# Paired projection loads, long decay reads, copies moved ahead, and half of the SSM output projection in split fp32r, in a hybrid decoder step on one core

## The chip, the core and the metric

The kernel runs on one core of one Trainium2 chip. The metric is the device time of one execution in microseconds; three executions of the kernel before give a median of 1370.95 us. Everything told below of the inside of an execution comes from one profiled execution.

## What is computed

One inference step of one layer for 256 prompt tokens and 8 sample tokens (264 rows, D_MODEL 1024, all float32): one wide input projection, a Mamba-2 state-space branch and a dilated window attention branch side by side, a gated sum of both, and a mixture of experts (top 4 of 32).

```python
def token_mixer(u, conv_buf, h0, kv_bufs, is_prompt, w_in, conv_w, conv_b, dt_bias, a_log, d_skip,
                ssm_norm_g, w_out_ssm, w_out_attn, w_out):
    proj = u @ w_in                                  # 9472 columns and dt
    z, xbc, dt_raw, q, k, v, gate_a, gate_b = jnp.split(proj, cuts, axis=-1)
    xbc_c = jax.nn.silu(causal_dwconv(xbc_ext, conv_w, conv_b))
    ...
    y, h_new = ssd_scan(xs, dt, A, Bm, Cm, h0)       # h0: (8, 32, 64, 128) for the samples
    y = (y + d_skip[:, None] * xs).reshape(Bsz, T, D_INNER) * jax.nn.silu(z)
    branch_a = group_rms_norm(y, ssm_norm_g) @ w_out_ssm          # 2048 x 1024
    ...                                              # attention: s = q k^T * scale - slope * dist, masked
    merged = jax.nn.sigmoid(gate_a) * branch_a + jax.nn.sigmoid(gate_b) * branch_b
    return merged @ w_out, new_conv, h_new, new_kv
```

Besides the result rows, the step returns the new convolution tail, the new sample states (8 MiB) and the sample caches moved on by one row: the latter is a plain copy of 44 MB in DRAM.

## The kernel before

**Projection (0 to 285 us).** w_in is taken in 37 units u of 256 columns. A unit is one 1 MiB load (L421) into `wraw`, a ring of RING = 5 places; its rows in DRAM are 1 KB long. A unit gives two tiles m = 2u, 2u+1 of 128 columns. A tile is made by ACT's rounded copy `high` (L799, into `wh`), the rest `wlow` by DVE (L1179) or GpSimd (L688), and 24 TensorE matmuls in fp32r (L1904 to L1906: xh by wh, xl by wh, xh by wlow). `tile_done` counts finished tiles. All weight loads are issued by SyncE (SP) from one list in program order; before the load of u it waits for `tile_done` >= 2(u-5)+2, which frees the place.

Between the loads the same list holds everything else that SP moves: a piece of the cache copy (`move_cache`, L432; 48 pieces, 40 of them of 1.05 MB, 8 of 0.26 MB), the broadcast reads of the decays (`decay_in`, L445: `a_scratch` in DRAM to `acb`, 0.5 MB), from u = 17 the sample inputs' round trip (`x_scratch` write L507, `xdts` read L509), and the sample states (`state_in` L462, `state_back` L467, 1 MiB each). An instruction of SP that waits holds all behind it.

**State-space phase, within the projection, from about 98 us.** Eight steps `it`, a group and a chunk each, run with the tiles from 26 on. For each sample b DVE makes the new state (L1324 once, then L1328, L1331) and reads it out (L1337, L1338). The states stand in `hs`, a ring of two: state_in(b) waits for the landing of state_back(b-2) (`hs_out`). PE's spread of the B and C rows of sample b waits for `hs_read` of b-1. The first of these DVE steps needs `xdts`, which has come back from DRAM.

**Attention and w_out_ssm (285 to 385 us).** `from_ssm(n)`, n = 0 to 15 (L2106), is a quarter of w_out_ssm's contraction for a pair of output tiles: four k, two column tiles, 8 float32 matmuls of 128x264 which the trace holds as 16 records. They are placed between the scores (L2089, L2090), the turned weights (L2122) and the products with the values (L2133 to L2135). Weights come by `native(i)` (L540) into `wnat`, again five places of 1 MiB. DVE adds a slope times distance (`bias`, L1436) to each head's scores (L1439), reduces them, and multiplies the sample queries with cached keys (L1486 to L1491); GpSimd scales the weights (L725). The masks are made at 256 to 272 us (L1391 to L1397). Values of the sample caches (`vsel`) are loaded by ACT (L971).

**Behind it.** `native(12)`, a quarter of w_out, waits for `native_used` = 8, that is for the end of from_ssm(15); behind it in SP's list stand the first weight chunks of the experts (L574, 2 MiB each). The output mix (L2243), norm and router follow to about 440 us, and the expert blocks to the end.

## Time and profile before

| | |
|---|---|
| median of 3 runs (lowest, highest) | 1370.95 us (1370.46, 1373.19) |
| profiled execution: time, span | 1370.5 us, 1368.8 us |
| granted clock, mean | 0.992 |
| PE, DVE, ACT, GpSimd busy | 1308.8, 574.5, 296.7, 169.9 us |
| DMA | 539.93 MB, mean 394 GB/s |

The span is the time from the first to the last instruction that the profiler saw; the 1.7 us between it and the execution's time lie around it. The shares are means over stages with different limits, so the stages above are read apart: the busy times in a window, the chain of work that ended last in it, and for a queue its issues in order of time.

### The profile page before, as it was taken

How to read it: one execution, taken by the hardware profiler on the slowest of the kernel's cores; microseconds unless marked ns; L12 is line 12 of the kernel's file. 1: busy time of each engine (PE TensorE's matmuls, PEld its weight loads, DVE VectorE, ACT ScalarE, POOL GpSimd, SP SyncE). 2: the span in 40 equal slices, each digit the busy share in tenths (PEclk: the TensorE clock that was granted, in tenths of full speed). 3: DMA queues.
4: the chain of work that ended last, by engine and by line, in shares of the span. 5: the costliest groups of instructions: out<-in, count | busy, mean ns of one | idle time of the engine just before them, and what ended most of it. 6: DMA issues, size and time to landing. Idle time of an engine off the chain costs nothing.

```text
span 1368.8 us, 24720 instructions
## 1 busy us (share of the span) xinstructions
PE 1308.8 (96%) x10213; PEld 653.0 (48%) x10213; DVE 574.5 (42%) x896; ACT 296.7 (22%) x603; POOL 169.9 (12%) x232
## 2 busy tenths in 40 slices
PE   9998999999999999999999999999999999999996
PEld 7998899976765333333333333333333322333322
DVE  4988999878457322132223221112222122222114
ACT  6778665643211100000000000000000000000002
POOL 1006774404000000000000000000000000000000
PEclk9999999999999999999999999999999999999998
DMA  8998998999999999999999999999999999999994
GB/s 269 338 386 258 359 364 294 380 345 383 400 375 369 396 424 428 425 427 427 429 426 427 428 427 429 424 428 424 428 427 428 428 427 427 426 429 425 431 424 189
DMA packets 113637, 539.93 MB, mean 394 GB/s; under 512 B 12901, under 2 KB 76501, under 8 KB 80773
## 3 DMA queue, kind: packets, MB, share of 16 engines
q1 hardware_dynamic: 103866, 524.91, 94.8%
q10 hardware_dynamic: 8448, 9.83, 2.2%
q0 software_dynamic: 1264, 4.35, 0.8%
q8 instruction: 44, 0.72, 0.2%
q14 instruction: 15, 0.12, 0.0%
HBM read 522.69 MB, written 60.56 MB: 426 GB/s over the span
## 4 chain that ended last, share of the span: by engine, by line
PE 64%; DMA 26%; DVE 6%; issue 2%; ACT 1%; POOL 1%; SPq 0%; ACTq 0%; DVEq 0%; POOLq 0%
PE psum L2394 21%; DMA wnat<-in_w_down_dram 10%; PE psum L2417 10%; DMA wmx<-in_w_down_dram 8%; DMA whm<-in_w_down_dram 6%; PE psum L2380 5%; PE psum L1904 4%; PE psum L1905 4%; PE psum L1906 4%; PE psum L2106 3%; PE psum L2440 3%; PE psum L2444 2%; PE psum L2243 1%; DMA x_scratch<-xbc 1%; PE psum L2425 1%
## 5 line engine op out<-in xcount | busy, mean ns | idle before, releaser
L1779 DVE STREAM_TRANSPOSE hturn<-psum 128x1024 f32<-128x1024 f32 x32 | 40.0, 1250 | 402.6 <-PE psum L2394 402.6
L1904 PE MATMUL psum<-xh,wh 128*128 128x264 f32 x592 | 173.1, 292 | 3.8 <-ACT zz L829 3.2
L1906 PE MATMUL psum<-xh,wlow 128*128 128x264 f32 x592 | 168.5, 285 | 0.0
L1905 PE MATMUL psum<-xl,wh 128*128 128x264 f32 x592 | 168.3, 284 | 0.0
L1116 ACT ACTIVATE sg<-hb 128x512 f32<-128x512 f32 x32 | 20.2, 631 | 523.5 <-DVE hb L1788 523.5
L2394 PE MATMUL psum<-wmh,xst 128*32 128x512 f32 x1056 | 118.6, 593 | 0.9 <-DVE xst L1745 0.8
L762 POOL COPY gcol<-gm 128x3 f32 (+1 forms) x32 | 17.4, 543 | 811.0 <-DVE hb L1783 810.3
L1904 PEld LDWEIGHTS psum<-xh,wh 128*128 128x128 f32 x592 | 112.3, 190 | 10.7 <-ACT zz L829 4.8
L1905 PEld LDWEIGHTS psum<-xl,wh 128*128 128x128 f32 x592 | 112.4, 190 | 1.4 <-issue 1.4
L1906 PEld LDWEIGHTS psum<-xh,wlow 128*128 128x128 f32 x592 | 111.7, 189 | 0.0
L2417 PE MATMUL psum<-wnat,hst 128*64 128x512 f32 x400 | 91.6, 598 | 14.3 <-DMA wnat<-in_w_down_dram 10.9
L2394 PE MATMUL psum<-spare,xst 128*32 128x512 f32 x816 | 95.1, 593 | 0.0
L2380 PE MATMUL psum<-x,oneh 128*32 128x256 f32 x1488 | 91.1, 390 | 0.0
L688 POOL TENSOR_TENSOR wlow<-wraw,wh 128x1024 fp32r<-128x1024 f32 x28 | 73.4, 2641 | 124.0 <-ACT wh L799 124.0
L2394 PE MATMUL psum<-wnat,xst 128*32 128x512 f32 x752 | 85.1, 592 | 0.0
L799 ACT ACTIVATE wh<-wraw 128x1024 fp32r<-128x1024 f32 x73 | 76.8, 1054 | 1.0 <-DMA wraw<-in_w_in_dram 1.0
L2380 PEld LDWEIGHTS psum<-x,oneh 128*32 128x32 f32 x1488 | 46.3, 108 | 54.2 <-issue 24.9
L2394 PEld LDWEIGHTS psum<-wmh,xst 128*32 128x32 f32 x1056 | 33.3, 110 | 75.5 <-issue 71.7
L1799 DVE TENSOR_TENSOR hst<-hu,sg 128x512 f32<-128x512 f32 x31 | 21.5, 693 | 110.4 <-PE psum L2417 110.4
L2417 PEld LDWEIGHTS psum<-wnat,hst 128*64 128x64 f32 x400 | 28.0, 136 | 77.7 <-issue 65.6
L2106 PE MATMUL psum<-zz,wnat 128*128 128x264 f32 x256 | 62.9, 400 | 0.0
L2440 PE MATMUL psum<-orow,gtok 64*128 64x512 f32 x248 | 61.6, 615 | 0.0
(459 smaller groups left out, 1733.2 us busy)
## 6 DMA issues: line engine op xcount, KB each, us to landing
wmh<-in_w_gate_up_dram SPq DMA_DIRECT2D x33, 2048.0 KB, 34.8
spare<-in_w_gate_up_dram SPq DMA_DIRECT2D x21, 2048.0 KB, 30.5
wnat<-in_w_gate_up_dram SPq DMA_DIRECT2D x20, 2048.0 KB, 36.9
wnat<-in_w_down_dram SPq DMA_DIRECT2D x20, 2048.0 KB, 34.8
wraw<-in_w_in_dram SPq DMA_DIRECT2D x37, 1024.0 KB, 9.9
out_dram<-in_cache_kv_w_dram SPq DMA_DIRECT2D x32, 1023.5 KB, 11.7
whm<-in_w_gate_up_dram SPq DMA_DIRECT2D x12, 2048.0 KB, 35.6
wmx<-in_w_gate_up_dram SPq DMA_DIRECT2D x11, 2048.0 KB, 37.5
```

The costliest lines, as they stand in the source:

```text
L688: g.tensor_tensor(half_of(wlow, m), half_of(wraw, m), high_of(m).bitcast(F32), ALU.subtract).then_inc(S("low_pool"), 1)
L799: a.activation(high_of(m), half_of(wraw, m), ACT.Copy).then_inc(S("high_done"), 1)
L1779: v.transpose(hturn[:, :].rearrange("p (f c i) -> p f c i", c=4, i=QW), psum[:, at:at + 2, :].rearrange("p h (f i c) -> p (h f) c i", c=4, ...
L1904: mm(out, hi[:, k, :], xh[:, k, :], start=(k == 0), stop=False)
L1905: mm(out, hi[:, k, :], xl[:, k, :], start=False, stop=False)
L1906: last = mm(out, lo[:, k, :], xh[:, k, :], start=False, stop=(k == KT - 1))
L2106: last = mm(bank[6 + odd][:, 0:T], w[:, k, odd * P:(odd + 1) * P], zz[:, KT * (r // 2) + k, :], start=(r == 0 and k == 0), stop=(r == 3 an ...
L2380: last = mm(bank[at][q * QW:(q + 1) * QW, 256 * h:256 * h + 256], rows_[:, t, h * QW:(h + 1) * QW], of_quarter(t, q), start=(t == 0), stop ...
L2394: last = mm(bank[at + h][q * QW:(q + 1) * QW, :], x_rows[:, h, k, :], w[:, q, :, :, :], start=(k == 0), stop=(k == KT - 1))
L2417: last = mm(bank[at][BLK * half:BLK * half + BLK, :], rows_[:, k, :, :].rearrange("p h r -> p (h r)"), w[:, col:col + 512], start=(k == 0) ...
L2440: last = mm(bank[3 + 2 * t + half], tok[rows_, t * P:(t + 1) * P], out[rows_, :], start=first, stop=final)
L2444: last = mm(bank[7][0:BLK, :], sam[:, :], out[:, :], start=first, stop=final)
```

## The change

1. *Paired loads.* For 2 <= u < 32 with u % 5 < 4, units (2,3), (5,6), (7,8), (10,11), ... (30,31) are one 2 MiB load, with DRAM rows of 2 KB; the others stay single. The place of a pair is two neighbours in the ring, so the pair's load waits until the *second* of the places is free.
2. *Long decay reads.* `a_scratch` is laid out so that a decay read is one 4 KB row per partition instead of eight of 512 B; it is written by four DMAs instead of one.
3. *Copies.* Every unit from 18 on has a piece of the cache copy (before: the even ones, and those above 33): 30 pieces instead of 22 are in the projection, 18 instead of 26 behind it (two instead of three behind native(0) to (4), one instead of two behind native(5) to (7)).
4. *w_out_ssm.* 8 of the 16 calls of `from_ssm` (n = 2, 3, 6, 7, 10, 11, 14, 15) are split: ACT rounds the weights (`wsh`) and, in two instructions, half of the normed rows (`zhi`); DVE makes the rests (`wlow`, `zlo`); PE does 24 fp32r matmuls instead of 8 float32 ones. from_ssm(8) stands before the loop over heads, and 9 to 11 one place later.
5. *Scores.* The masks hold the distance, and the slope goes into the scale of the exponential, so the 12 `bias` instructions go.
6. *Sample values* (`vsel`) are loaded by GpSimd behind its 12 scalings of `pa`, after `qk_done` 8. Some buffers lie elsewhere, and some semaphores are merged.

```diff
+        def load_of(u):
+
+            return u - u % RING % 2 if 2 <= u < 32 and u % RING < 4 else u
+
+        def units_of(u):
+
+            return 2 if load_of(u + 1) == u else 1
+
+        def raw_ready(eng, u):
+
+            n = load_of(u)
+            loads = sum(load_of(v) == v for v in range(n % RING, n + 1, RING))
+            eng.wait_ge(S(f"raw_landed{n % RING}"), 16 * loads)
...
@@ -441,8 +497,8 @@
                 gi, c = divmod(it, 2)
                 if it >= 3:
                     sp.wait_ge(S("ssd_y"), it - 2)
-                src = a_scratch[gi * HPG:(gi + 1) * HPG, c * P:(c + 1) * P].unsqueeze(0).broadcast_to([P, HPG, P])
-                sp.dma_start(acb[:, it % 3, :, :], src).then_inc(S(f"acb_in{it % 3}"), 16)
+                src = a_scratch[gi, c].rearrange("h l -> (h l)").unsqueeze(0).broadcast_to([P, HPG * P])
+                sp.dma_start(acb[:, it % 3, :, :].rearrange("p h l -> p (h l)"), src).then_inc(S(f"acb_in{it % 3}"), 16)
...
                 if u >= RING:
-                    sp.wait_ge(S("tile_done"), 2 * (u - RING) + 2)
-                    if 5 < u < 17 or u > 33 or (u >= 18 and u % 2 == 0):
+                    before = u + units_of(u) - 1 - RING
+                    sp.wait_ge(S("tile_done"), 2 * (load_of(before) + units_of(load_of(before)) - 1) + 2)
+                    if 5 < u < 17 or u > 17:
                         move_cache(next(pieces))
-                load(u, wraw[:, u % RING, :].rearrange("p (k n) -> p k n", k=KT), w_in_v[:, :, w_in_col(u):w_in_col(u) + 256])
+                if load_of(u) == u:
+                    load(u, raw_place(wraw, u), w_in_v[:, :, w_in_col(u):w_in_col(u) + 256 * units_of(u)])
...
-                    sp.wait_ge(S("a_out"), 16)
+                    sp.wait_ge(S("a_out"), 16 * GROUPS)
...
             for i in range(RING):
                 native(i)
-                for _ in range(3):
+                for _ in range(2):
                     move_cache(next(pieces))
...
             for i in range(RING, N_SSM + N_ATT + N_OUT):
                 native(i)
                 move_cache(next(pieces))
-                if i < N_SSM:
-                    move_cache(next(pieces))
```

In attention and w_out_ssm:

```diff
+        SSM_SPLIT = (2, 3, 6, 7, 10, 11, 14, 15)
...
+            def ssm_split(n):
+
+                native_ready(act, n // 2)
+                at = SSM_SPLIT.index(n)
+                if at == 2:
+                    act.wait_ge(*reached("rstd_ready"))
+                elif at > 2:
+                    ssm_used(act, SSM_SPLIT[at - 3])
+                a.activation(ssm_high(n), ssm_part(wnat, n), ACT.Copy).then_inc(S("high_done"), 1)
...
+                own.then(v.scalar_tensor_tensor(out=mk, in0=mk, scalar=NEG, in1=rel[:, :], op0=ALU.mult,
+                                                op1=ALU.subtract))
...
+            def norm_low(gi):
+
+                high_ready(dve, f"z{gi}")
+                v.tensor_tensor(zlo[:, 4 * gi:4 * gi + 4, :], zz[:, 4 * gi:4 * gi + 4, :],
+                                zhi[:, 4 * gi:4 * gi + 4, :].bitcast(F32), ALU.subtract).then_inc(S("low_done"), 1)
+
+            def ssm_low(n):
+
+                high_ready(dve, f"w{n}")
+                v.tensor_tensor(ssm_part(wlow, n), ssm_part(wnat, n), ssm_high(n).bitcast(F32),
+                                ALU.subtract).then_inc(S("low_done"), 1)
...
-                bs = bias[:, h % 2, :]
-                own.then(v.scalar_tensor_tensor(out=bs, in0=rel[:, :], scalar=-SLOPES[h], in1=masks[:, h // HG, :],
-                                                op0=ALU.mult, op1=ALU.add))
+                if h in (1, 3):
+                    norm_low(2 + h // 2)
+                elif h in (2, 4):
+                    ssm_low(1 + h // 2)
+                elif h == 8:
+                    ssm_low(6)
                 dve.wait_ge(S("scores_psum"), h + 1)
-                v.scalar_tensor_tensor(out=pa[:, h, :], in0=bank[4 + h % 2][:, 0:3 * P], scalar=SCALE, in1=bs,
-                                       op0=ALU.mult, op1=ALU.add).then_inc(S("score_read"), 1)
+                v.scalar_tensor_tensor(out=pa[:, h, :], in0=bank[4 + h % 2][:, 0:3 * P], scalar=SCALE / SLOPES[h],
+                                       in1=masks[:, h // HG, :], op0=ALU.mult, op1=ALU.add).then_inc(S("score_read"), 1)
                 dve.wait_ge(S("score_read"), h + 1)
...
+                if n in SSM_SPLIT:
+                    low_ready(pe, f"w{n}")
+                    hi, lo = (w.rearrange("p (k n) -> p k n", k=4) for w in (ssm_high(n), ssm_part(wlow, n)))
+                else:
+                    native_ready(pe, n // 2)
+                    w = ssm_part(wnat, n).rearrange("p (k n) -> p k n", k=4)
                 for odd in range(2):
-                    for k in range(4 * (r % 2), 4 * (r % 2) + 4):
-                        last = mm(bank[6 + odd][:, 0:T], w[:, k, odd * P:(odd + 1) * P], zz[:, KT * (r // 2) + k, :],
-                                  start=(r == 0 and k == 0), stop=(r == 3 and k == KT - 1))
-                if r % 2:
-                    last.then_inc(S("native_used"), 1)
+                    out, cols = bank[6 + odd][:, 0:T], slice(odd * P, (odd + 1) * P)
+                    for k in range(4):
+                        f = 4 * r + k
+                        if n not in SSM_SPLIT:
+                            last = mm(out, w[:, k, cols], zz[:, f, :], start=(f == 0), stop=False)
+                            continue
+                        mm(out, hi[:, k, cols], zhi[:, f, :], start=(f == 0), stop=False)
+                        mm(out, hi[:, k, cols], zlo[:, f, :], start=False, stop=False)
+                        last = mm(out, lo[:, k, cols], zhi[:, f, :], start=False, stop=(f == ZT - 1))
+                last.then_inc(S("native_used" if r % 2 else "half_used"), 1)
...
+            from_ssm(8)
             keys = [min(P, PAST // d) for _, d in DIL]
             for n in range(NH + 1):
                 if n == 4:
@@ -2181,7 +2282,7 @@
                     weights_turn(n)
                 if n:
                     weights_times_v(n - 1)
-                if n in (2, 5, 8, 11):
+                if n in (3, 6, 9):
                     from_ssm(8 + n // 3)
```

SP's list around the sample inputs' round trip (x_scratch), before: the loads are u = 15, then 16, then 17, then 18.

```order
L432 DMA out_dram<-in_cache_kv_w_dram 16x16352 [waits tile_done]
L421 DMA wraw<-in_w_in_dram 128x8x256
L421 DMA wraw<-in_w_in_dram 128x8x256 [waits tile_done]
L507 DMA x_scratch<-xbc 128x16x8 [waits conv_done]
L509 DMA xdts<-x_scratch 128x128 [waits xs_out]
L432 DMA out_dram<-in_cache_kv_w_dram 16x4064 [waits tile_done]
L421 DMA wraw<-in_w_in_dram 128x8x256
```

And of the change, from the pair (15, 16) to the copy of u = 18:

```order
L488 DMA out_dram<-in_cache_kv_w_dram 16x16376 [waits tile_done]
L477 DMA wraw<-in_w_in_dram 128x8x512
L488 DMA out_dram<-in_cache_kv_w_dram 16x16352 [waits tile_done]
L477 DMA wraw<-in_w_in_dram 128x8x512 [waits tile_done]
L565 DMA x_scratch<-xbc 128x16x8 [waits conv_done]
L567 DMA xdts<-x_scratch 128x128 [waits xs_out]
L488 DMA out_dram<-in_cache_kv_w_dram 16x4064 [waits tile_done]
```

The load ahead of `x_scratch` is now the pair (17, 18), and it waits for tile 27; before it was the single u = 17, which waited for tile 25.

SP's list at the sample states, before: from the load of u = 20 to that of u = 23, with the states 2 in, 1 back and 3 in.

```order
L421 DMA wraw<-in_w_in_dram 128x8x256
L462 DMA hs<-in_state_ssm_dram 128x2048 [waits hs_out0,hs_read]
L421 DMA wraw<-in_w_in_dram 128x8x256 [waits tile_done]
L445 DMA acb<-a_scratch 128x8x128 [waits ssd_y]
L467 DMA out_dram<-hs 128x2048 [waits hnew_ready]
L432 DMA out_dram<-in_cache_kv_w_dram 16x16376 [waits tile_done]
L421 DMA wraw<-in_w_in_dram 128x8x256
L462 DMA hs<-in_state_ssm_dram 128x2048 [waits hs_out1,hs_read]
L421 DMA wraw<-in_w_in_dram 128x8x256 [waits tile_done]
```

And of the change, from the copy of u = 20 (the loads are (20, 21) and (22, 23)):

```order
L488 DMA out_dram<-in_cache_kv_w_dram 16x16376 [waits tile_done]
L477 DMA wraw<-in_w_in_dram 128x8x512
L518 DMA hs<-in_state_ssm_dram 128x2048 [waits hs_out0,hs_read]
L488 DMA out_dram<-in_cache_kv_w_dram 16x16376 [waits tile_done]
L501 DMA acb<-a_scratch 128x1024 [waits ssd_y]
L523 DMA out_dram<-hs 128x2048 [waits hnew_ready]
L488 DMA out_dram<-in_cache_kv_w_dram 16x16376 [waits tile_done]
L477 DMA wraw<-in_w_in_dram 128x8x512
L518 DMA hs<-in_state_ssm_dram 128x2048 [waits hs_out1,hs_read]
```

State 3 in (the last row) now stands behind a copy and a pair that wait for `tile_done` 38; before, behind a copy and a single load that waited for 36.

ACT's list in the attention stage, before: the end of the prompt's softmax (L1007, L1009), then the scalings (L1015) and the copies of the turned weights (pT, L1029).

```order
L1007 ACT_TABLE_LOAD
L1007 ACTIVATE ast<-ast 128x24 [waits aexp_done]
L1009 ACT_TABLE_LOAD
L1009 ACTIVATE ast<-ast 128x24 [waits dve_stage]
L1015 ACTIVATE pa<-pa,ast 128x128 [waits dve_stage]
L1015 ACTIVATE pa<-pa,ast 128x128 x2
L1029 ACTIVATE pT<-psum 128x384 [waits pturn_psum]
L1015 ACTIVATE pa<-pa,ast 128x128
```

And of the change: the roundings for from_ssm(10), (11) and (14) (L1041) stand in it.

```order
L1078 ACT_TABLE_LOAD
L1078 ACTIVATE ast<-ast 128x24 [waits aexp_done]
L1041 ACTIVATE wsh<-wnat 128x1024 [waits native_used,native_landed2]
L1081 ACT_TABLE_LOAD
L1081 ACTIVATE ast<-ast 128x24 [waits dve_stage]
L1087 ACTIVATE pa<-pa,ast 128x128 [waits dve_stage]
L1087 ACTIVATE pa<-pa,ast 128x128
L1041 ACTIVATE wsh<-wnat 128x1024 [waits half_used,native_landed2]
L1041 ACTIVATE wsh<-wnat 128x1024 [waits native_used,native_landed4]
L1087 ACTIVATE pa<-pa,ast 128x128
L1100 ACTIVATE pT<-psum 128x384 [waits pturn_psum]
```

The rounding for from_ssm(10) stands ahead of the softmax's last exponential, those for 11 and 14 ahead of the first pT, and each waits for its piece of w_out_ssm: native(5) (`native_landed2`) and native(7) (`native_landed4`).

## Rows read from the trace of the kernel before

**Rows 1.** Windows: busy us by engine, TensorE clock, DMA share, GB/s
```profile
106.00:108.00 2.00, 1.62 (x14) 1.41 (x12) 1.23 (x1) 1.97 (x3) 0.00 (x0) 1.00 0.66 112
120.00:220.00 100.00, 97.33 (x854) 89.59 (x853) 99.44 (x81) 66.31 (x124) 78.79 (x29) 1.00 1.02 353
320.00:380.00 60.00, 58.72 (x350) 44.38 (x348) 32.24 (x81) 14.34 (x33) 12.84 (x14) 1.00 1.04 407
...
480.00:1340.00 860.00, 828.54 (x6641) 273.41 (x6636) 199.16 (x272) 55.20 (x150) 41.85 (x116) 1.00 1.01 427
```

**Rows 2.** Chain that ended last, 285 to 395 us: start, us, what
```profile
288.40 3.76 PE psum L2106 x16
...
308.92 0.56 DVE bias L1436
...
329.04 3.76 PE psum L2106 x16
...
363.48 0.71 DVE gates L1425
...
385.22 9.54 DMA wnat<-in_w_out_dram
```

**Rows 3.** The same chain at 96 to 112 us
```profile
96.18 1.96 SPq L421
98.18 11.93 DMA x_scratch<-xbc
110.12 1.81 DMA xdts<-x_scratch
```

**Rows 4.** PE in order of time, first work behind tile 27
```profile
103.44 1.06 PE L2007 MATMUL psum<-bcrow,ident 32*32 32x256 f32 x16
```

**Rows 5.** SP in order of time: start, us of issue, what
```profile
146.59 0.35 SPq L462 DMA_DIRECT2D hs<-in_state_ssm_dram  x1
150.66 0.37 SPq L421 DMA_DIRECT2D wraw<-in_w_in_dram  x1
...
168.88 2.53 SPq L467 DMA_DIRECT2D out_dram<-hs  x1
175.34 0.52 SPq L432 DMA_DIRECT2D out_dram<-in_cache_kv_w_dram  x1
...
178.62 0.34 SPq L462 DMA_DIRECT2D hs<-in_state_ssm_dram  x1
```

**Rows 6.** DMA issues at 146 to 147 us: KB each, us to landing
```profile
hs<-in_state_ssm_dram SPq DMA_DIRECT2D x1, 1024.0 KB, 9.5
```

**Rows 7.** DMA issues at 16 to 17 us, nothing queued ahead
```profile
wraw<-in_w_in_dram SPq DMA_DIRECT2D x1, 1024.0 KB, 5.4
```

**Rows 8.** DVE in order of time: the start and three sample states
```profile
112.03 2.39 DVE L1324 TENSOR_TENSOR xdts<-xdts,feat 128x128 f32<-128x128 f32 x1 [1.49 <-DMA xdts<-x_scratch]
...
116.78 2.35 DVE L1331 SCALAR_TENSOR_TENSOR hs<-hs,feat,sprod 128x2048 f32<-128x2048 f32 x1
...
161.00 3.48 DVE L1331 SCALAR_TENSOR_TENSOR hs<-hs,feat,sprod 128x2048 f32<-128x2048 f32 x1
...
192.91 3.87 DVE L1331 SCALAR_TENSOR_TENSOR hs<-hs,feat,sprod 128x2048 f32<-128x2048 f32 x1
```

**Rows 9.** Groups by line: busy us, mean ns, idle before and releaser
```profile
L1179 DVE TENSOR_TENSOR wlow<-wraw,wh 128x1024 fp32r<-128x1024 f32 x45 | 55.8, 1260 | 5.3 <-ACT wh L799 5.2
...
L1439 DVE SCALAR_TENSOR_TENSOR pa<-psum,bias 128x384 f32<-128x384 f32 x12 | 6.7, 557 | 7.7 <-PE psum L2090 7.5
L1436 DVE SCALAR_TENSOR_TENSOR bias<-rel,masks 128x384 f32<-128x384 f32 x12 | 6.6, 552 | 0.0
```

**Rows 10.** PE in order of time: one tile, 25 records of a steady stretch
```profile
59.74 0.28 PE L1904 MATMUL psum<-xh,wh 128*128 128x264 f32 x1
...
62.64 0.28 PE L1904 MATMUL psum<-xh,wh 128*128 128x264 f32 x1
```

**Rows 11.** DVE in order of time: the last step of a mask
```profile
260.48 0.36 DVE L1397 TENSOR_SCALAR masks<-masks 128x384 f32<-128x384 f32 x1
```

More of the change, by code:

```diff
@@ L590, in _ @@
             for m in range(10):
[L591 to L593 removed]
+                if m == 2:
                     sp.wait_ge(S("native_used"), N_SSM)
@@ L1246, in convolve @@
                     if m < CW - 1:
-                        steps.then(last)
+                        own.then(last)
                 t = ctmp[:, u % 3, :, TP:T]
```

163 lines of the change are left out of this document (98 added, 65 removed).

## The prediction

> **What bounds the kernel now.** I read the windows first, then the chain of waits, then the queues in order of time. The windows [rows 1] show three regimes. At 120 to 220 us everything is full: PE 97.33 and DVE 99.44 of 100 us, DMA share 1.02 at 353 GB/s. At 320 to 380 us PE is busy 58.72 of 60. From 480 us on DMA has share 1.01 at 427 GB/s, so the expert stage can't be shortened from here; it can only start sooner or later. Its gate is in the chain [rows 2]: behind the end of from_ssm(15) at 385.22 us comes the wait of 9.54 us for a piece of w_out, and the first expert chunks are issued behind that piece. So the kernel's end moves with the end of from_ssm(15), microsecond for microsecond. Fewer bytes ahead of that gate don't move it, since it is PE's. The change therefore has to be summed over two stretches: the projection (to 285 us) and attention with w_out_ssm (285 to 385 us).
>
> **Attention and w_out_ssm.** *Split products.* A call of from_ssm takes 3.76 us (16 records) [rows 2]. 24 fp32r matmuls of the same width take 62.64 - 59.74 = 2.90 us [rows 10]. That is 0.87 us less, and 8 x 0.87 = 7.0 us of PE's time. But the chain is on DVE from about 307 us (a `bias` step at 308.92) to 329.04 [rows 2]. Ahead of it, n = 2 and 3 bring the scores 1.7 us sooner. In the DVE stretch the splits of n = 6 and 7 are hidden; DVE loses four `bias` steps (chain at 308.92 and its like, 0.55 us each by [rows 9]: -2.2) and gets two `ssm_low` of the kind of L1179, 1.26 us [rows 9]: +2.5. Together -1.7 - 2.2 + 2.5 = **-1.4 us**. The other eight `bias` steps lay in DVE's waits for PE (L1439 waits 7.5 us for L2090 [rows 9]), and the four other rests (2 x 1.3 and 2 x 1.26 = 5.1 us) go where they were. From 329 us PE bounds, and n = 10, 11, 14, 15 give 4 x 0.87 = **-3.5 us**, if their halves are ready. ACT makes each from a piece that must have landed; if it is late, ACT holds the exponential and the copies queued behind it, and DVE and PE wait for these. One or two MB less behind each native piece make it likely that (5) and (7) are in time; a piece that is 2 us late costs 2 us. from_ssm(8) to (11) moved ahead of DVE's waits: the chain's piece at 363.48 (gates, 0.71 us [rows 2]) is partly filled, **-0.5 us**. Sum: -5.4. Bounds: all PE time saved and the gap filled, 7.0 + 1.5 = -8.5; only the four late ones, half of them on time, and the lows exposed, -3.
>
> GpSimd's loads of the sample values start behind its scalings, some 22 us later than ACT's first; their reader at 372 us is still 15 us or more behind the landing. I take 0; if it fails, it costs the same wait at from_ssm(14), at most 3 us. DVE's rests now run beside GpSimd. L1331 takes 2.35 us at 116.78 and 3.48 at 161.00 [rows 8], where GpSimd is busy most of the time (78.79 of 100 us [rows 1]). The Trainium skill, "SBUF - State Buffer", section "Who interferes with whom", says why: a DVE instruction with two SBUF inputs and a GpSimd instruction that reads SBUF exclude each other. By it `ssm_low(10)`, which meets the scalings at 325 to 337 us, could wait for one of them, 1 us; the sum does without.
>
> The masks' last step becomes one with two inputs: 0.55 (as L1436 [rows 9]) for 0.36 [rows 11], three times, +0.6 us, on the chain at 256 to 272 us.
>
> **Projection, what is removed.** Rows of 2 KB and 4 KB. A 1 MiB load with nothing ahead lands in 5.4 us [rows 7]; the full queue moves 353 GB/s with short rows, 427 with long ones [rows 1]. Between these a MiB costs 2.97 or 2.46 us, so a pair saves between 0 and 1.0 us of the queue. 12 pairs: 0 to 12 us of DMA time, the decays' reads another 0 to 3. Against it stand 8 more copy pieces in u = 19 to 33, 6 x 1.05 + 2 x 0.26 = 6.8 MB, 19 us at 353 GB/s, where the share is 1.02 already. So the queue is by 4 to 19 us busier there, not freer. The Trainium skill ("DMA: Bandwidth & Descriptors", section "Anatomy of one DMA") gives about 2.0 us plus bytes by 436 GB/s for a DMA issued by GpSimd. By it a pair takes 6.8 us where two single loads in a row take 8.8, and the change would win. The trace speaks for it only where the queue is empty, and there it is not.
>
> **Projection, what is added: waits.** A pair waits for its second place, two tiles later than its first unit did, and what stands behind it on SP waits too.
>
> (a) *Start.* The pair (2,3) lands as one. The first two slots' tiles wait for 2 MiB instead of 1: 2.5 us at 427 GB/s, of which ACT's other work hides a part. **+1.5 us** (0 to 2.5).
>
> (b) *x_scratch.* Before, SP issued u = 17 at 96.18, x_scratch at 98.18, landing 11.93 us later, and xdts follows at 110.12 with 1.81 [rows 3]; DVE starts at 112.03 after idling [rows 8]. The queue's payload ended near 106.6, as the 112 GB/s at 106:108 shows [rows 1]: x_scratch lands 3.5 us behind it. In the change the pair (17,18) waits for tile 27, and the first PE work behind tile 27 is at 103.44 [rows 4]. 2 MiB at 353 to 427 GB/s is 4.9 to 5.9 us, with 2 us to its start (5.4 less the 2.5 to 3 us of its bytes) it ends at 110.3 to 111.4. +3.5 for x_scratch, +1.9 for xdts gives 116.3, against 112.03: **+4.3 us** (3 to 6). DVE has no idle time from here to 220 us, so nothing takes it back. What is late next: PE's spread for samples 1 and on, all in step.
>
> (c) *States.* State 3 in is issued at 146.59 behind tile_done 36 and lands after 9.5 us [rows 5, 6], at 156.1; DVE uses it at 161.00 [rows 8]: 4.9 us of slack. In the change it stands behind tile_done 38, when SP took u = 23 before (150.66 [rows 5]), and behind a copy and 2 MiB, 3.1 MB or 7.4 to 8.9 us, and its own 1 MiB, 2.5 to 3: 161.9 to 163.5 plus up to 2 of landing: +1 to +4.5. State 3 back goes from 168.88 to behind 175.34, +6.5, and state 5 in needs its landing (178.62 before [rows 5]). 178.62 + 6.5 + 9.5 = 194.6, against the use at 192.91 [rows 8]: +1.7, more if queues are longer. State 6: +0.7 to 2.8 in the same way. PE is within 3% of being the bound here and can run ahead by one sample, so some of it is won back: **+3.5 us** (0 to 8).
>
> Projection: 1.5 + 4.3 + 3.5 + 0.6 = **+9.9 us** (3 to 17).
>
> **Sum.** 9.9 - 5.4 = +4.5 us on the profiled execution's 1370.5: **1375.0 us**. That execution is 0.45 us under the median of 1370.95, less than the runs' own spread.
>
> **The rivals.**
> A, *delays outweigh the splits* (forecast): 1372 to 1379, from +7 to +14 in the projection.
> B, *faster*. The delays are absorbed: the queue, emptier at 98 to 104 us by the pair's late issue, takes the 2 MiB at once, and long rows keep the states' latencies below 9.5 us, so that state 3 meets its 4.9 us. Left are 1.5 + 0.6 and at most 1.5 of (b): 1370.5 + 3.6 - 5.4 = 1368.7, with the ends of the gains 1365 to 1362.5. It decides if xdts lands before 113.5 us and DVE keeps its 99% at 120 to 220. For it: a pair's two units are there in one piece, and PE can wait little. Against it: x_scratch's fixed place behind tile 27. This is also where the skill's rule of "DMA: Bandwidth & Descriptors" points.
> C, *they cancel*: (b) in full, no state late: 1.5 + 4.3 + 0.6 - 5.4 = +1.0, 1371.5.
> D, *the queue is the bound*: the 19 us of added copies come back as late states at each of three turns, and ACT waits for weights at 250 us: +17 - 5.4, 1382.
> That the change does not do what it says I exclude for the splits and the order: the lists show them.
>
> **Chances.** A 0.44, B 0.33, C 0.13, D 0.10. A measurement of this kernel can tell about 0.2%, 2.7 us. Faster than 1368.2: 0.32 (B nearly whole); within: 0.21 (C and A's low end); slower than 1373.7: 0.47. The range 1362.5 to 1384 leaves out the tails of B and D. Since B has another sign, A's own range: 1371 to 1380.
>
> **What would show it.** x_scratch issued near 104.5 and DVE's L1324 at 116, not 112. DVE idle for `hs` ahead of its fourth and sixth L1331; DVE under 97% at 120 to 220 us. DMA over 353 GB/s there. End of the projection (the first scores) near 295 instead of 285. 8 calls of from_ssm at 2.9 us, and from there to the w_out wait 95 us instead of 100. The experts' stage unchanged in length. Wrong would be: no idle of DVE for states (then B or C), a gain under 3 us behind the projection (ACT held by a native piece), or an expert stage of other length.

## The result and the profile after

The changed kernel takes **1391.85 us** (median of 4 runs, 1391.47 to 1394.32) for 1370.7 us; the ratio is 1.0154 (1.0136 to 1.0172). It is slower by 21 us. I had forecast 1375.0 and a range of 1362.5 to 1384: the sign was right and the size was far too small.

Windows of the changed kernel (busy us of PE, PEld, DVE, ACT, GpSimd, then TensorE's clock, DMA share, GB/s):

```profile
22.00:30.00 8.00, 6.85 (x56) 6.51 (x55) 3.60 (x5) 4.65 (x7) 0.00 (x0) 1.00 0.60 201
30.00:60.00 30.00, 27.95 (x221) 27.51 (x220) 27.32 (x62) 21.18 (x41) 0.00 (x0) 0.94 0.73 265
125.00:235.00 110.00, 105.25 (x885) 97.50 (x886) 94.05 (x83) 70.68 (x130) 78.16 (x29) 0.95 0.94 346
330.00:335.00 5.00, 5.00 (x14) 3.76 (x15) 4.72 (x16) 3.52 (x13) 3.11 (x4) 0.53 1.29 465
480.00:1340.00 860.00, 828.19 (x6654) 271.84 (x6644) 203.13 (x275) 55.86 (x151) 44.77 (x124) 1.00 1.01 426
```

The kernel before, in the first two of these:

```profile
22.00:30.00 8.00, 8.00 (x68) 7.71 (x65) 5.10 (x8) 7.85 (x16) 0.00 (x0) 1.00 1.10 348
30.00:60.00 30.00, 29.53 (x246) 29.14 (x246) 28.32 (x61) 23.07 (x43) 0.00 (x0) 1.00 1.01 343
```

The row 480:1340 answers to that in [rows 1]: share 1.01 at 426 GB/s for 427, so the expert stage is as it was. At 22 to 60 us the DMA queue is not full any more: share 0.60 and 0.73 for 1.10 and 1.01. At 125 to 235 us DVE is busy 94.05 of 110 us; the kernel before had it at 99.44 of 100 at 120 to 220 us. The share is 0.94 there, though there was more to move.

SP of the changed kernel in order of time, with the places that answer to [rows 3] and [rows 5]:

```profile
107.65 0.38 SPq L477 DMA_DIRECT2D wraw<-in_w_in_dram  x1
108.07 0.58 SPq L565 DMA_DIRECT2D x_scratch<-xbc  x1
119.08 0.34 SPq L567 DMA_DIRECT2D xdts<-x_scratch  x1
...
141.67 0.54 SPq L488 DMA_DIRECT2D out_dram<-in_cache_kv_w_dram  x1
142.25 0.58 SPq L477 DMA_DIRECT2D wraw<-in_w_in_dram  x1
142.94 0.51 SPq L518 DMA_DIRECT2D hs<-in_state_ssm_dram  x1
...
145.23 0.45 SPq L523 DMA_DIRECT2D out_dram<-hs  x1
...
163.62 0.33 SPq L518 DMA_DIRECT2D hs<-in_state_ssm_dram  x1
```

The pair (17,18) is issued at 107.65 where I had put it at 104, and the write of the round trip behind it has landed by 119.08 for 110.12. In the state ring, write-back 1 goes at 145.23 and state 3 can only be asked for at 163.62. These are the DMA pieces of over 8 us in the chain that ended last, from 16 to 300 us (start, us, what):

```profile
16.36 9.36 DMA wraw<-in_w_in_dram
...
77.28 12.11 DMA wraw<-in_w_in_dram
...
95.04 14.51 DMA wraw<-in_w_in_dram
...
145.23 18.33 DMA out_dram<-hs
...
163.62 10.40 DMA hs<-in_state_ssm_dram
...
205.28 14.72 DMA out_dram<-hs
...
221.68 14.66 DMA out_dram<-hs
...
236.40 8.33 DMA hs<-in_state_ssm_dram
...
254.72 9.51 DMA y_scratch<-ysum
```

Up to 110 us the chain waits three times for weights, and the round trip of x_scratch is not in it; then it goes through the ring of states, and at the end through a second round trip (y_scratch, the samples' y), whose write takes 9.51 us to land. The write-back at 145.23 takes 18.33 us to land (8.9 to 12.5 for the eight of the kernel before), behind a copy, a 2 MiB load, a state, a second copy and a decay read, all issued within 4 us ahead of it. Who waited on DMA in the first 300 us, DVE first, then ACT (total, times, longest):

```profile
DVE hs L1403 <- DMA hs<-in_state_ssm_dram: 19.8, 5, 4.9
...
DVE xbc L1444 <- DMA ysf<-y_scratch: 5.0, 1, 5.0
```

```profile
ACT wh L858 <- DMA wraw<-in_w_in_dram: 32.0, 11, 6.0
```

In the kernel before, DVE waited neither for a state nor for `ysf`, and ACT once, 1.0 us, for weights. Now DVE waits 19.8 us for states and ACT 32.0 us for weights.

TensorE's clock fell too. It was granted at the lower of its two levels (1.2 of 2.4 GHz) in several stretches, each behind one in which PE had waited; one of them, from 126 us on, is in the chain:

```profile
124.00:128.00 4.00, 1.72 (x8) 1.73 (x9) 4.00 (x3) 3.97 (x6) 0.76 (x1) 0.68 0.63 165
128.00:132.00 4.00, 4.00 (x20) 4.00 (x20) 3.96 (x4) 0.43 (x2) 3.96 (x2) 0.50 0.69 258
```

Added up over windows of 1 us from 18 us to the first score, the granted clock is short of full speed by 12.0 us in the changed kernel, and by 1.7 us in the kernel before. What this adds to the time, beside the waits ahead of it, no run parts.

The traces of all kernels split the time at two places: the first score (L2089 before, L2183 after), and the issue of the last piece of w_out, which SP may do at the end of from_ssm(15).

| kernel | projection, to the first score | first score to end of from_ssm(15) | from there to the end |
|---|---|---|---|
| before | 285.1 | 100.1 | 983.6 |
| changed | 306.9 | 101.1 | 984.6 |

These lengths are of one profiled execution each; that of the changed kernel was its slowest, 1394.32 us for a median of 1391.85. The projection lost 21.8 us. The attention stage, in which I had expected -5.4, lost 1.0. The rest is rigid, as forecast.

### The profile page after: what moved, and what is told of

It reads as the page before. It is cut to its first block, busy times and chain, and to the rows that moved or that the text cites. A ratio compares the mean times of both kernels' runs of the same rounds, so it can differ in the third digit from the quotient of the medians.

```text
span 1392.6 us, 24840 instructions
## 1 busy us (share of the span) xinstructions
PE 1314.6 (94%) x10277; PEld 661.4 (47%) x10277; DVE 571.5 (41%) x894; ACT 306.5 (22%) x613; POOL 169.1 (12%) x235
## 4 chain that ended last, share of the span: by engine, by line
PE 56%; DMA 34%; DVE 5%; ACT 2%; issue 2%; SPq 1%; ACTq 0%; DVEq 0%
PE psum L2495 21%; DMA wnat<-in_w_down_dram 10%; PE psum L2518 9%; DMA wmx<-in_w_down_dram 8%; DMA wmh<-in_w_down_dram 6%; PE psum L2481 5%; DMA out_dram<-hs 3%; PE psum L2541 3%; DMA wraw<-in_w_in_dram 3%; PE psum L1998 2%; PE psum L1999 2%; PE psum L2000 2%; PE psum L2204 2%; PE psum L2545 2%; DMA hs<-in_state_ssm_dram 1%
## 5 line engine op out<-in xcount | busy, mean ns | idle before, releaser
L1998 PE MATMUL psum<-xh,wh 128*128 128x264 f32 x592 | 177.3, 300 | 11.2 <-ACT zz L888 4.0
L1999 PE MATMUL psum<-xl,wh 128*128 128x264 f32 x592 | 171.9, 290 | 0.0
L2000 PE MATMUL psum<-xh,wlow 128*128 128x264 f32 x592 | 171.7, 290 | 0.0
L1998 PEld LDWEIGHTS psum<-xh,wh 128*128 128x128 f32 x592 | 115.8, 196 | 18.9 <-ACT zz L888 5.6
L2495 PE MATMUL psum<-wmh,xst 128*32 128x512 f32 x1088 | 122.0, 593 | 2.7 <-DMA wmh<-in_w_gate_up_dram 1.0
L1999 PEld LDWEIGHTS psum<-xl,wh 128*128 128x128 f32 x592 | 116.1, 196 | 1.4 <-issue 1.4
L2000 PEld LDWEIGHTS psum<-xh,wlow 128*128 128x128 f32 x592 | 115.4, 195 | 0.0
L1253 DVE TENSOR_TENSOR wlow<-wraw,wh 128x1024 fp32r<-128x1024 f32 x45 | 54.2, 1231 | 7.6 <-ACT wh L858 7.4
## 6 DMA issues: line engine op xcount, KB each, us to landing
wraw<-in_w_in_dram SPq DMA_DIRECT2D x12, 2048.0 KB, 11.3
```

The source lines that it names most:

```text
L1253: v.tensor_tensor(half_of(wlow, m), half_of(wraw, m), high_of(m).bitcast(F32), ALU.subtract).then_inc(S("low_done"), 1)
L1998: mm(out, hi[:, k, :], xh[:, k, :], start=(k == 0), stop=False)
L1999: mm(out, hi[:, k, :], xl[:, k, :], start=False, stop=False)
L2000: last = mm(out, lo[:, k, :], xh[:, k, :], start=False, stop=(k == KT - 1))
L2495: last = mm(bank[at + h][q * QW:(q + 1) * QW, :], x_rows[:, h, k, :], w[:, q, :, :, :], start=(k == 0), stop=(k == KT - 1))
```

## Experiments

Two stages, so two questions: what in the projection costs 22 us, and where the split products' gain went. The kernels whose names begin with a are the changed one with something undone, those with b the kernel before with something added. The first four undo or do the pairs and the moved copies. A median is compared with that of the kernel before run beside it (1369.9 to 1370.8 us). The lengths of stages and the waits are of one profiled execution, which lies up to 4.2 us from its kernel's median: above it by 3.1 us in b_pairs_first, 4.2 in b_pairs_last and in b_pairs_x, 4.1 in a_late, below it by 2.6 in a_single_late and 2.1 in a_both.

**a_single**

```diff
         def load_of(u):
-            return u - u % RING % 2 if 2 <= u < 32 and u % RING < 4 else u
+            return u
```

> The changed kernel with single 1 MiB projection loads, each waiting for its own place only (the pairing undone); the 8 moved copies, the long decay reads and everything in the attention stage stay. The change lost 21 us against the kernel before; all of it is in the projection, where the first score stands at 306.9 us for 285.1. Theory P (the pairs' waits and bursts starve the ring of two states): the projection ends near 286 to 289 us and the time is 1371 to 1376, and no L1403 waits for DMA longer than 1 us. Theory C (the 6.8 MB of copies overload a full queue): the state waits stay, 1386 to 1390. Theory B (it takes both): 1377 to 1384.

1377.52 us (1373.62 to 1381.07), ratio to before 1.0046 (1.0025 to 1.0066). 14.3 of the 21 us come back with the pairs. Still 8.1 us of waits for states in three places, so the copies have a part of their own.

**a_copies**

```diff
-                    if 5 < u < 17 or u > 17:
+                    if 5 < u < 17 or u > 33 or (u >= 18 and u % 2 == 0):
                         move_cache(next(pieces))
...
                 native(i)
-                for _ in range(2):
+                for _ in range(3):
...
                 move_cache(next(pieces))
+                if i < N_SSM:
+                    move_cache(next(pieces))
```

> The changed kernel with the cache copies where they were before (22 pieces in the projection, 26 behind it); the pairs stay. Theory P: 1385 to 1390, little regained. Theory C: 1372 to 1376. Theory B: 1377 to 1384. In each, the landing of a state's write-back (14.7 to 18.3 us in the changed kernel, 8.9 to 12.5 before) says how much was queued ahead of it.

1396.07 us (1395.42 to 1400.14): 4 us slower than the changed kernel, which none of the theories had. The two places in its trace say why: first score at 299.1 (7.8 us sooner than changed), but 110.5 us from there to the end of from_ssm(15) for 101.1. The copies are a cost in the projection and a gain behind it; a_both shows the second part more clearly.

**a_both**: both edits.

> The changed kernel with both undone: single loads and the copies as before. What is left is the long decay reads, the split products, the folded slope and the sample values by GpSimd. If the projection is as before, the time is the attention stage's alone: the traces give +1.0 us for it (101.1 us from the first score to the end of from_ssm(15) for 100.1), so 1371 to 1373; my prediction said -5.4 for it, 1366.

1375.22 us (1373.09 to 1376.26), ratio 1.0034 (1.0023 to 1.0045). First score at 282.1, which is 3 us *sooner* than before; then 105.3 us for 100.1. ACT of this kernel in order of time, its roundings for from_ssm(6), (7), (10) and (11) (start, duration, and in brackets the idle time ahead and what ended it):

```profile
298.18 1.06 ACT L1043 ACTIVATE wsh<-wnat 128x1024 fp32r<-128x1024 f32 x1 [7.40 <-DMA wnat<-in_w_out_ssm_dram]
...
303.54 1.04 ACT L1043 ACTIVATE wsh<-wnat 128x1024 fp32r<-128x1024 f32 x1
...
322.48 1.06 ACT L1043 ACTIVATE wsh<-wnat 128x1024 fp32r<-128x1024 f32 x1 [11.11 <-DMA wnat<-in_w_out_ssm_dram]
...
327.01 1.04 ACT L1043 ACTIVATE wsh<-wnat 128x1024 fp32r<-128x1024 f32 x1
```

ACT stands 7.40 and 11.11 us for a piece of w_out_ssm that has not landed. Behind the second stands the last exponential of the softmax; DVE waits for it and PE for DVE, 6.5 us in one piece by PE's list of waits. So with the copies where they were, the change to the attention stage as a whole loses 5.2 us; the moved copies are what makes room for the pieces.

**b_pairs**: the pairs alone, on the kernel before, with the waits and the places of the change.

```diff
-                    sp.wait_ge(S("tile_done"), 2 * (u - RING) + 2)
+                    before = u + units_of(u) - 1 - RING
+                    sp.wait_ge(S("tile_done"), 2 * (load_of(before) + units_of(load_of(before)) - 1) + 2)
...
+                if load_of(u) == u:
+                    load(u, raw_place(wraw, u), w_in_v[:, :, w_in_col(u):w_in_col(u) + 256 * units_of(u)])
```

> The kernel before with the paired loads and nothing else. Theory P: at least three quarters of the projection's loss, +15 us or more, 1386. Theory C: +1 to +5. Theory B: +5 to +12. My prediction's own terms for this part, 1.5 + 4.3 + 3.5 = +9.3, give 1380.

1386.68 us (1385.37 to 1387.92), ratio 1.0118 (1.0102 to 1.0135): +16.0 us, theory P. First score at 299.0, attention 100.1 as before.

**The waits or the transfers.**

b_two_loads:

```diff
                 if load_of(u) == u:
-                    load(u, raw_place(wraw, u), w_in_v[:, :, w_in_col(u):w_in_col(u) + 256 * units_of(u)])
+                    for v in range(u, u + units_of(u)):
+                        load(v, wraw[:, v % RING, :]..., w_in_v[:, :, w_in_col(v):w_in_col(v) + 256])
```

> The kernel before, whose loads wait as the pairs do (for the second place, and what stands behind them in SP's list too), but each pair is two single 1 MiB loads, one right behind the other, each with its own semaphore. Paired loads alone took 1386.7 us for 1370.7. Theory W (the later waits of SP cost it): nearly the same loss, 1382 to 1388. Theory L (the pair lands only as a whole, so ACT gets its first tile late): most comes back, 1371 to 1375. If half each: 1376 to 1381. Rows of 1 KB instead of 2 KB would make it slower by up to 0.5 us a MiB where the queue is full.

1383.48 us (1382.0 to 1385.22), +13.6 of the 16 us (the kernel before beside it took 1369.9). Theory W: most is the waiting for the second place. The other 2.4 us are not clear of noise (1.01, 1.0082 to 1.0117, for 1.0118, 1.0102 to 1.0135). They fit a transfer that lands only as a whole, since ACT waits 16.6 us for weights here and 23.0 in b_pairs, but no run shows that this is their cause; in any case the 2 KB rows gained nothing.

**Which waits.** Three kernels look into b_pairs by place.

b_pairs_first and b_pairs_last change the range of the pairs in b_pairs:

```diff
-            return u - u % RING % 2 if 2 <= u < 32 and u % RING < 4 else u
+            return u - u % RING % 2 if 2 <= u < 15 and u % RING < 4 else u
```

with `20 <= u < 32` in the second. b_pairs_x issues the write of the round trip ahead of the wait for the pair (17,18):

```diff
+                if u == 17:
+                    with nc.allow_non_contiguous_dma(reason="eight tokens"):
+                        sp.wait_ge(S("conv_done"), 12)
+                        sp.dma_start(by_feature(x_scratch), xbc[:, X0:X0 + ZT, TP:T]).then_inc(S("xs_out"), 16)
                 if u >= RING:
                     before = u + units_of(u) - 1 - RING
...
-                        sp.wait_ge(S("conv_done"), 12)
-                        sp.dma_start(by_feature(x_scratch), xbc[:, X0:X0 + ZT, TP:T]).then_inc(S("xs_out"), 16)
                         sp.wait_ge(S("xs_out"), 16)
```

> The kernel before with pairs only for u = 2 to 13; no state and no round trip stands behind one of their waits. All pairs: +16 us. Theory F (the ring of five weight places, refilled by twos, lets ACT and PE run dry in the first 100 us): +6 to +10, 1376 to 1380. Theory S (the loss is in what stands behind the waits, states and round trip): +1.5 to +3, 1371.5 to 1373, the start alone, as I had predicted.

1376.55 us (1375.1 to 1379.61), +6.6 us: theory F for this part. Its ACT, in order of time:

```profile
25.37 1.06 ACT L819 ACTIVATE wh<-wraw 128x1024 fp32r<-128x1024 f32 x1 [3.02 <-DMA wraw<-in_w_in_dram]
...
59.77 1.07 ACT L819 ACTIVATE wh<-wraw 128x1024 fp32r<-128x1024 f32 x1 [2.84 <-DMA wraw<-in_w_in_dram]
...
78.23 1.06 ACT L819 ACTIVATE wh<-wraw 128x1024 fp32r<-128x1024 f32 x1 [3.85 <-DMA wraw<-in_w_in_dram]
...
90.72 1.06 ACT L819 ACTIVATE wh<-wraw 128x1024 fp32r<-128x1024 f32 x1 [3.68 <-DMA wraw<-in_w_in_dram]
...
100.38 1.06 ACT L819 ACTIVATE wh<-wraw 128x1024 fp32r<-128x1024 f32 x1 [1.31 <-DMA wraw<-in_w_in_dram]
...
108.07 1.06 ACT L819 ACTIVATE wh<-wraw 128x1024 fp32r<-128x1024 f32 x1 [3.20 <-DMA wraw<-in_w_in_dram]
```

> The kernel before with pairs only for u = 20 to 31, where the states move. My prediction's term for the states was +3.5 (0 to 8). Theory F: 1371 to 1376. Theory S: +8 to +12, 1378 to 1382. The weights should be in time here, since a tile takes 4 us of PE and DVE for 2.9 in the first 95 us.

1377.13 us (1375.07 to 1381.37), +7.2 us, just under theory S (+8), with 8.8 us of DVE's waits for states in four places, and 4.9 us of ACT's for weights:

```profile
DVE hs L1351 <- DMA hs<-in_state_ssm_dram: 8.8, 4, 5.8
```

> The kernel before with all pairs, and the write of the round trip (x_scratch) issued ahead of the wait and load of the pair (17,18). My price for its delay was 4.3 us: 1386.7 - 4.3 = 1382.4 if it is on the path that sets the end. If PE and ACT, short of weights, are as late as DVE by then, the round trip is covered: 1385 to 1387.

1383.64 us (1382.03 to 1387.88): +13.7 for b_pairs' +16.0, each against the kernel before beside it. These 2.3 us are not clear of noise (1.0097, 1.0081 to 1.0112, for 1.0118, 1.0102 to 1.0135), and the traces speak against them: in b_pairs_x SP asks for xdts at 113.62 and DVE waits for it no more, but DVE's first product with it (`sprod`) starts at 121.17 for 121.60 in b_pairs, and neither chain holds the round trip; both wait for weights up to 109.7 us. So with all pairs the round trip is covered.

The pairs below u = 15 and those from 20 on make 6.6 + 7.2 = 13.8 of the 16.0 us. The other 2.2 belong to the pairs (15,16) and (17,18), which neither kernel has, if the parts add up. Each stretch in which SP stood for a second place lost time, the first of them before any state moved.

**The order of the copies.** If the pieces of the cache copy harm by standing ahead of the states, they may stand behind them:

```diff
-                    if 5 < u < 17 or u > 17:
+                    if 5 < u < 17:
                         move_cache(next(pieces))
...
                 elif u >= 20 and u < 20 + 2 * (TS - HSN):
                     state_in((u - 16) // 2)
+                if u > 17:
+                    move_cache(next(pieces))
```

This edit on a_single is a_single_late, and on the changed kernel a_late.

> Single loads and the moved copies as in a_single (1377.5 us), but from u = 18 on each copy is issued behind that unit's load, decay read and state transfers instead of ahead of them: the same bytes and the same waits in another order. Theory Q (what stands ahead of a state's transfer in SP's list and in its queue delays it): the waits of L1403 for states fall from 8.1 us to under 2, the projection ends 3 to 6 us sooner, 1372 to 1374.5. Theory R (the bytes alone, a full DMA queue): no gain, 1376 to 1379, since the queue is as full.

1371.94 us (1369.36 to 1375.32), ratio 1.0012 (1.0 to 1.0024): 5.6 us less than a_single from the order alone. No DVE step waits for a state, and at 120 to 220 us:

```profile
120.00:220.00 100.00, 97.33 (x847) 89.93 (x847) 99.02 (x85) 66.37 (x124) 78.66 (x29) 0.98 1.03 392
```

392 GB/s, for 353 in [rows 1], with DVE at 99.02. The added bytes went through. The first score stands at 284.7 us for 290.8 in a_single, and 282.1 in a_both without the moved copies: of the 8.7 us that they cost, 6.1 were the order, and 2.6 are left (by one trace each, and that of a_single_late is its fastest).

> The changed kernel (paired loads, moved copies) with the same reordering of the copies from u = 18 on. Theory Q: the copy was 1 MB of the 4 to 5 MB ahead of a state; the pair's 2 MiB and its later wait stay, so about a third of the 21 us comes back, 1384 to 1388. If the pairs' loss is mostly ACT's waits for weights (32.0 us in eleven waits in the changed kernel, 1.0 before), which the copies behind make no better, 1389 to 1393.

1390.09 us (1386.89 to 1394.14): 1.8 us less than the changed kernel, within the noise. With the pairs, ACT still waits 29.7 us for weights and DVE 18.6 for states; the copies' order is not what holds them.

**The attention stage.**

a_single_from8, on a_single:

```diff
                 if b % 2:
                     from_ssm(4 + b // 2)
-            from_ssm(8)
...
-                if n in (3, 6, 9):
+                if n in (2, 5, 8, 11):
                     from_ssm(8 + n // 3)
```

> a_single with from_ssm(8) to (11) at the places of the kernel before (n = 2, 5, 8, 11 of the head loop). In a_single PE waits 3.0 us for the gated sum (L1511) at from_ssm(8), and runs 1.4 us slower behind it at a lower clock. If that place is the cost: -3 to -4.5 us, 1373 to 1374.5. If DVE's later steps bind the stretch anyway: within 1 us of 1377.5.

1375.53 us (1374.33 to 1376.2), 2.0 us less; the stage takes 98.6 us for a_single's 100.8. The new places of from_ssm(8) to (11) were a cost of about 2 us. The two intervals overlap (1.0021 to 1.0043, 1.0025 to 1.0066), but a_best below finds the same 2 us again.

a_single_nosplit, on a_single, all 16 calls in float32, with no roundings and rests:

```diff
-        SSM_SPLIT = (2, 3, 6, 7, 10, 11, 14, 15)
+        SSM_SPLIT = ()
```

> a_single with all 16 calls of from_ssm in float32 matmuls: no ACT roundings and no DVE rests for w_out_ssm; order of calls, folded slope and the rest stay. By my prediction's price of 0.87 us a call, with those for n = 6, 7 hidden and n = 2, 3 half, it is 4 to 5 us slower than a_single: 1382. By the trace of a_single a split call stands for 3.12 us (303.34 to 306.46), 0.64 less than 3.76, and its rests cost DVE 1.2 us each in a stretch that DVE bounds: only n = 10, 11, 14, 15 pay, 2.6 us, and six rests and roundings give back 2.4 to 3.7: 1376 to 1378, the same as a_single.

1378.65 us (1376.51 to 1380.48), with 1377.52 within its range. In the profiled executions the stage takes 103.8 us for 100.8, in the medians the whole differs by 1.1, which is within the noise. My terms for the splits with DVE's rests came to 2.7 us (1.7 - 2.5 + 3.5). The chain of this kernel, from_ssm(4) and (13), both float32:

```profile
317.41 5.91 PE psum L2211 x16
...
376.36 5.44 PE psum L2211 x16
```

**What is left, and a faster kernel.**

a_plain: the changed kernel with the edits of a_single, a_copies, a_single_from8 and a_single_nosplit together.

> The changed kernel without pairs, moved copies, split products and the new places of from_ssm(8) to (11): what is left over the kernel before is the long decay reads, the folded slope with the masks, and the sample values by GpSimd. Long reads alone: 1367.8. My terms for the rest: four bias steps on the path, -2.2 us, and +0.6 for the masks: 1366.2. If PE or the other DVE steps take the place of the bias steps: 1367.5 to 1368.5.

1368.34 us (1367.09 to 1371.08), ratio 0.9992 (0.9983 to 1.0001).

b_reads: the kernel before with item 2 of the change alone.

```diff
-        a_scratch = nc.dram_tensor("a_scratch", (HEADS, TP), F32, kind="Internal").ap()
+        a_scratch = nc.dram_tensor("a_scratch", (GROUPS, 2, HPG, P), F32, kind="Internal").ap()
...
-                src = a_scratch[gi * HPG:(gi + 1) * HPG, c * P:(c + 1) * P].unsqueeze(0).broadcast_to([P, HPG, P])
+                src = a_scratch[gi, c].rearrange("h l -> (h l)").unsqueeze(0).broadcast_to([P, HPG * P])
```

> The kernel before with the long decay reads (4 KB rows instead of 512 B) and nothing else. In a_both the first score stands at 282.1 us for 285.1, and the reads are the only difference in the projection. If they did it: -3 us, 1367.7. If the 3 us was an accident of where the transfers fell: 1370 to 1371.

1367.77 us (1367.0 to 1368.26), ratio 0.9984 (0.9975 to 0.9993): 2.1 us faster than the kernel before. First score at 281.7; DVE's first sample step starts at 110.22 for 112.03, its second state update at 124.15 for 130.23. Only 1.8 of these 6.1 us are the earlier start; two DVE steps between them take 0.29 and 1.22 us where they took 2.39 and 3.39 in the kernel before, and no run shows why.

b_reads_late: b_reads, with its copies from u = 18 on behind the state transfers, by the edit of a_single_late.

> b_reads with the copies of the cache (as many and in the same units as before) issued behind the state transfers from u = 18 on. In the kernel before no DVE step waits for a state, so theory Q, by which the order pays only where states are late, gives nothing more than b_reads: 1367 to 1369. Should it be over 1 us faster than b_reads, the copies also delayed something else, such as the weights.

1367.39 us (1366.36 to 1369.93), ratio 0.9982 (0.9973 to 0.9991): nothing beyond b_reads, as theory Q says where no state is late.

a_best: a_single_late with the edit of a_single_from8.

> a_single_late (1371.9 us: single loads, the moved copies behind the state transfers from u = 18) with from_ssm(8) to (11) at the places of the kernel before. The two edits are in different stages and each has been measured: -5.6 and -2.0 us against a_single's 1377.5. If they add up: 1369.9, the kernel before within the noise or 0.5 to 1 us under it. If ACT's wait for a piece of w_out_ssm (3.9 us in a_single_late) takes the second's place: 1371 to 1372.

1369.83 us (1368.89 to 1372.9), ratio 1.0 (0.9991 to 1.0009): the two edits add up, as expected. Single loads, moved copies behind the states and the split products are worth the kernel before, no more.

| kernel | projection | attention | median us |
|---|---|---|---|
| a_single | 290.8 | 100.8 | 1377.5 |
| a_copies | 299.1 | 110.5 | 1396.1 |
| a_both | 282.1 | 105.3 | 1375.2 |
| b_pairs | 299.0 | 100.1 | 1386.7 |
| b_two_loads | 296.8 | 100.1 | 1383.5 |
| b_pairs_first | 294.0 | 100.4 | 1376.6 |
| b_pairs_last | 292.6 | 100.5 | 1377.1 |
| b_pairs_x | 300.8 | 100.4 | 1383.6 |
| a_single_late | 284.7 | 99.1 | 1371.9 |
| a_plain | 282.2 | 98.3 | 1368.3 |
| b_reads | 281.7 | 100.4 | 1367.8 |
| a_best | 284.6 | 98.4 | 1369.8 |

## Why the prediction was wrong

**What bounds the kernel: right.** In 18 profiled executions the stretch behind from_ssm(15) is 983 to 987 us long whatever came ahead of it. The losses could be summed over two stretches.

**The projection: right that it loses, too small in size, and one of three paths wrong.** I had +9.9 us; it was 21.8. By the experiments (projection column): long reads -3.0 (a_both against before), pairs +16.1 (a_single to changed) or +17.0 (a_both to a_copies), copies +7.8 or +8.7. By my terms:

(a) *Start*, +1.5 us: the step that failed worst. I looked at the first pair alone and asked how long 2 MiB take. The pairs below u = 15 cost 6.6 us. Each waits until its second place is free, so the weights come late for one pair after another: ACT waits in six places of b_pairs_first, 17.9 us in all, and the DMA share falls to 0.57 at 22 to 30 us. I had let ACT's other work hide a part, and never set the issue of each pair against the time of its first use; the ring of five, with a landing of 9.9 us, had little to give.

(b) *x_scratch*, +4.3: the wrong path. DVE's first sample step does start late, at 120.95 for 112.03, but not through the pair that I blamed: in b_pairs_first, which has no pair there, it starts at 119.63, since x_scratch is only issued at 109.35 for 98.18, by its chain:

```profile
109.35 8.30 DMA x_scratch<-xbc
117.66 1.87 DMA xdts<-x_scratch
```

With all pairs the chain holds the landing of weights in its place (14.51 us from 95.04). The delay came out of (a), and my sum had it as a term of its own.

(c) *States*, +3.5 (0 to 8): the mechanism was right, the size not. Pairs from u = 20 cost 7.2 us, and the moved copies another 8. I took the landing times of the kernel before (9.5 us) and moved the issues. But a landing holds the queue ahead, and that grew with both: write-backs took 11.4 to 18.3 us for 8.9 to 12.5, and five of eight states were late by 3.4 to 4.9 us each. The round trip of y_scratch, for which I had no term, made DVE wait 5.0 us more, in the chain. No run shows anything "won back". Two sums in these terms are wrong as well: 150.66 with 7.4 to 8.9 and 2.5 to 3 us is 160.6 to 162.6, not 161.9 to 163.5, and in (b) 5.4 less 2.5 to 3 leaves 2.4 to 2.9 us to a load's start, not 2. Put right, the first is about 1 us less and the second 0.4 to 0.9 us more, which leaves the forecast about where it was.

Last, the sum had no term for TensorE's clock, which in the projection was short of full speed by 12.0 us for 1.7; how much of the loss that is stays open. In b_pairs it was 5.1 us, 3.4 more than before, while the projection grew by 13.9, so it is the smaller part there.

The long reads, which I had only as 0 to 3 us of DMA time in a queue that the copies fill again, brought the first score forward by 3 us, and the median by 2.1.

The bytes: I held the queue to be full by the share of 1.02 and to have 4 to 19 us more work. a_single_late moved them at 392 GB/s, for 2.6 us. So 353 GB/s at a share of 1.02 was no ceiling. The Trainium skill ("DMA: Bandwidth & Descriptors", section "Bandwidth") asks to batch to 1 MiB or more for at least 75% of peak; the loads were at 1 MiB already, and b_two_loads against b_pairs shows no gain of going to 2 MiB: 1383.5 for 1386.7.

**Attention: wrong in size, and in its sum.** PE of a_single in order of time, the first split call and the score behind it:

```profile
303.34 0.32 PE psum L2206
...
306.46 0.43 PE psum L2183 x4
```

A split call stands for 306.46 - 303.34 = 3.12 us in the chain, so 0.64 us less than 3.76 and not 0.87: I took 24 matmuls inside a steady stretch of one kind, and left out what stands at a change of kind. Eight calls are 5.1 us less of PE's time, not 7.0. The chain of the changed kernel, at three places of the stage, with two float32 calls:

```profile
332.69 5.95 PE psum L2204 x16
...
354.62 0.63 DVE gates L1511
...
391.55 5.44 PE psum L2204 x16
```

And PE's waits of that kernel in the stage (total, times, longest):

```profile
PE psum L2204 <- DVE gates L1511: 3.0, 1, 3.0
...
PE psum L2294 <- DVE sst L1630: 1.5, 1, 1.5
```

I part the stage where from_ssm(8) to (15) and the head loop begin: at 355.3 us in the changed kernel and 332.8 in the kernel before. *The first half* takes 48.4 us for 47.7, and I had expected -1.4. The splits of n = 2 and 3 bring DVE's turn in the chain 1.3 us sooner; those of n = 6 and 7 lie beside DVE's steps, as forecast. Two things took it back. From 329.99 to 339.19 us the chain is on PE at the lower clock (0.53 at 330 to 335 us, behind 5 us in which PE was busy for 3.35), with from_ssm(4) at 5.95 us, where before it was on DVE. And from_ssm(8) must now wait for the gated sum (L1511), which DVE does behind `ssm_low(10)`: PE stands for 3.0 us, where I had booked -0.5 for this move. a_single_from8 gives 2.0 us of that back; the first of the two no run parts. *The second half* takes 52.7 us for 52.4, and I had expected -3.5: four splits give -2.6, PE's wait for the sample softmax (L2294) is 1.5 us for 0.3, and the float32 call at 391.55, behind that wait, takes 5.44 us for 3.76; together +0.3.

The splits are not the cause of the slow calls: a_single_nosplit has none, and its calls at 317.41 and 376.36 take 5.91 and 5.44 us. In the kernel before, too, from_ssm(4) takes 5.51 us, but beside DVE:

```profile
311.65 5.51 PE L2106 MATMUL psum<-zz,wnat 128*128 128x264 f32 x16
```

In both kernels PE had waited for others just before (busy 2.39 of 4 us at 308 to 312 before, 4.46 of 6 at 370 to 376 in a_single_nosplit), and my sum took each call at full clock.

The folded slope takes the stage from 100.4 to 98.3 us (b_reads against a_plain, both with long reads, one trace each), about my -2.2; in the medians of the whole kernel it does not show, 1368.3 for 1367.8. Neither DVE nor PE waited for the sample values, as forecast. That ACT's halves would be in time because the copies were moved was right: in the changed kernel ACT waits 0.7 us for a piece of w_out_ssm in the stage, in a_both 7.4, 11.1 and 11.3.

**Rivals.** B fell with its own test (xdts after 113.5 us). D named late states at each turn and ACT's waits for weights, at 1382 and a chance of 0.10; its waits were what happened, but they came with the pairs and with the order of the copies more than with its cause, the bytes. All four cases rested on the same three places in the projection, so none could reach 1392.

## What to carry to other kernels

A transfer that is merged with its neighbour also merges their waits: it starts when the *last* of its places is free, and on an in-order queue everything behind it starts then too. Set the issue of every such transfer, not of the first, against its first use, and take a landing time from the queue that the change makes, not from the one that was. Put bulk copies behind the transfers that a ring waits for: with single loads the same bytes cost 2.6 us of the projection in that order, and 8.7 in the other. Where TensorE waits more, look for its clock in the windows too: here it was lower for longer.

## What the runs showed of the hardware

At 120 to 220 us the DMA engines moved 392 GB/s in a_single_late at a share of 1.03, and 353 in the kernel before at 1.02: the share alone did not say that no more would fit. Reading 0.5 MB per decay in rows of 4 KB for 512 B is worth 2.1 us of the kernel's time (b_reads), though the reads were never waited for; the write of x_scratch behind them has landed by 108.01 us for 110.12. A call of eight float32 matmuls takes 3.76 us at TensorE's full clock and 5.4 to 6.0 us where the clock is at its lower level for most of it; 24 fp32r matmuls of the same width take 3.12 us in its place.
